# The last attention of two blocks: scores and values as products of rounded high and low parts

## What is computed

```python
def gqa_attend(q, k, v, sink=None):
    s = jnp.einsum('bqhgd,bkhd->bhgqk', q.reshape(b, tq, hkv, g, d), k).astype(jnp.float32) * d ** -0.5
    if sink is None:
        p = jax.nn.softmax(s, axis=-1)
    o = jnp.einsum('bhgqk,bkhd->bqhgd', p.astype(v.dtype), v)

# c_mixer: q_l, k_l rotated; k_all, v_all are context and latent tokens together (768)
    q_blocks = jnp.moveaxis(q_l.reshape(b, t // BLOCK, BLOCK, C_HEADS, C_HEAD_DIM), 1, 0)
    o = lax.map(lambda qb: gqa_attend(qb, k_all, v_all), q_blocks)
    y_lat = jnp.moveaxis(o, 0, 1).reshape(b, t, C_WIDTH) @ w_out
```

## Time and profile before

| | us |
|---|---|
| median of 3 runs | 2615.78 (2614.35 to 2617.09) |
| the profiled execution | 2614.36 |
| its span | 2612.6 |
| PE busy | 2381.1 (91%) |
| PE weight loads | 1929.9 (74%) |
| DVE busy | 1231.2 (47%) |
| ACT busy | 805.5 (31%) |
| POOL busy | 1003.8 (38%) |
| mean granted clock of PE | 0.954 |

### The profile page before, as it was taken

One profiled execution on the slowest core, in us unless ns is written; L12 is line 12 of the kernel. 1 busy time (PEld: TensorE's weight loads), 2 busy tenths in 40 slices (PEclk: granted clock), 3 DMA queues, 4 the chain that ended last, 5 costly groups with the idle time before them and its releaser, 6 DMA issues. The chain is left out here.

```text
span 2612.6 us, 34942 instructions
## 1 busy us (share of the span) xinstructions
PE 2381.1 (91%) x14323; PEld 1929.9 (74%) x14323; DVE 1231.2 (47%) x1956; ACT 805.5 (31%) x1325; POOL 1003.8 (38%) x606
## 2 busy tenths in 40 slices
PE   6987688999997989967789999999989998899998
PEld 5866466777775779855668888888867687688887
DVE  4417627756555660567436242332427752423432
ACT  4232334333335412335332111111134363322221
POOL 3326234655553322320136343443434002555553
PEclk8998898999997999979899999999989999899999
DMA  8570213444441111100113233333311101233221
GB/s 266 161 226 1 75 49 113 157 153 154 149 145 58 40 48 59 33 1 1 33 49 97 81 113 114 114 127 100 113 41 65 33 1 49 65 97 97 96 97 49
DMA packets 224700, 229.94 MB, mean 88 GB/s; under 512 B 7375, under 2 KB 221219, under 8 KB 224547
## 3 DMA queue, kind: packets, MB, share of 16 engines
q1 hardware_dynamic: 224211, 227.66, 27.1%
q10 hardware_dynamic: 336, 0.11, 0.0%
HBM read 225.65 MB, written 2.10 MB: 87 GB/s over the span
## 5 line engine op out<-in xcount | busy, mean ns | idle before, releaser
L1237 POOL TENSOR_TENSOR w_lo<-ring,w_hi 128x1024 fp32r<-128x1024 f32 x128 | 311.5, 2434 | 431.5 <-ACT w_hi L1232 431.5
L1232 ACT ACTIVATE w_hi<-ring 128x1024 fp32r<-128x1024 f32 x128 | 135.6, 1059 | 738.4 <-PE ps L1297 701.9
L2039 DVE SCALAR_TENSOR_TENSOR xT<-ps,mods,xT 128x512 f32<-128x512 f32 (+1 forms) x160 | 108.3, 683 | 533.0 <-PE ps L1297 474.0
L1295 PE MATMUL ps<-hidden_hi,w_hi 128*128 128x512 f32 (+1 forms) x768 | 273.9, 357 | 5.4 <-POOL hidden_lo L2393 5.4
L1296 PE MATMUL ps<-hidden_lo,w_hi 128*128 128x512 f32 (+1 forms) x768 | 272.1, 354 | 0.0
L1297 PE MATMUL ps<-hidden_hi,w_lo 128*128 128x512 f32 (+1 forms) x768 | 271.6, 354 | 0.0
L2316 DVE SCALAR_TENSOR_TENSOR ffn_sums<-ps,cols,ffn_sums 128x441 f32<-128x441 f32 (+2 forms) x352 | 215.0, 687 | 105.5 <-ACT ffn_sums L2237 105.5
L1295 PE MATMUL ps<-h_hi,w_hi 128*128 128x512 f32 (+1 forms) x720 | 256.4, 356 | 6.7 <-POOL w_lo L1237 3.0
L1296 PE MATMUL ps<-h_lo,w_hi 128*128 128x512 f32 (+1 forms) x720 | 255.0, 354 | 0.0
L1297 PE MATMUL ps<-h_hi,w_lo 128*128 128x512 f32 (+1 forms) x720 | 254.6, 354 | 0.0
L2383 DVE TENSOR_TENSOR squares<-squares 128x512 f32<-128x512 f32 (+1 forms) x72 | 144.9, 2013 | 217.7 <-ACT squares L2369 217.7
(11 more groups left out here) (448 smaller groups left out, 5223.7 us busy)
## 6 DMA issues: line engine op xcount, KB each, us to landing
ring<-in_mlp_w SPq DMA_DIRECT2D x64, 1024.0 KB, 5.3
ring<-in_ada_w SPq DMA_DIRECT2D x48, 1024.0 KB, 5.3
ring<-in_w_ada SPq DMA_DIRECT2D x24, 1024.0 KB, 9.6
ring<-in_ffn_w_up SPq DMA_DIRECT2D x22, 1024.0 KB, 7.0
ring<-in_ab_w_in SPq DMA_DIRECT2D x11, 1024.0 KB, 5.2
ring<-in_ffn_w_down SPq DMA_DIRECT2D x12, 768.0 KB, 6.0
ring<-in_w_in SPq DMA_DIRECT2D x8, 1024.0 KB, 7.5
ring<-in_c_w_in SPq DMA_DIRECT2D x6, 1024.0 KB, 5.0
```

The lines of the kernel that those rows point to most:

```text
L1232: act.activation(w_hi[m][:, 0:x["kt"], :], ring[:, x["n"] % NS, 0:x["kt"], m * P:(m + 1) * P], ACT.Copy).then_inc(SW["w_hi"].sem, 1)
L1237: pool.tensor_tensor(w_lo[m][:, 0:x["kt"], :], ring[:, x["n"] % NS, 0:x["kt"], m * P:(m + 1) * P], w_hi[m][:, 0:x["kt"], :].bitcast(F32), ...
L1295: pe.matmul(o, w_hi[m][:, k, :], h, start=(k == 0), stop=False)
L2039: return nc.vector.scalar_tensor_tensor(x, bank, column_of(gates, t * 2 + 2 * gate + r), x, ALU.mult, ALU.add)
```

## The change

`attention` becomes `split_attention`. The jobs and their order stay. Heads 1 to 7 make their scores from rounded parts, three products for each column range; head 0 keeps the float32 products. The values are made from rounded parts for two jobs (query blocks) at a time, with 256 columns. ACT's copy of the transposes, now rounded, is the high part `p_hi`; a new step `low(j)` on DVE subtracts it from the transposes in PSUM and writes `p_lo`, after `norm(j+1)` in DVE's queue. `turn(j)` waits for that step of job j-1 (`turned_v`) too. ACT rounds k, v and q of each head (`part_high`) at set steps of its loop, and POOL subtracts (`part_lo`). The low parts of q, k (but the first head's) and v are written over the originals. `scores(4h)` waits for the low parts of its head, `values` for those of v.

```diff
+            ops = [("v", 0), ("k", 0), ("q", 1), ("q", 2), ("v", 1), ("k", 1)] + [("q", h) for h in range(3, 8)]
+            when = {("v", 0): -1, ("k", 0): 0, ("v", 1): 7, ("k", 1): 8}
+            when.update({("q", h): 4 * h - 3 for h in range(1, 8)})
...
                 @block.gpsimd
                 def _(pool):
-                    for dst, factor in side:
-                        pool.tensor_tensor(dst, dst, factor, ALU.mult)
+                    for i, (kind, index) in enumerate(ops):
+                        x, hi, lo = tiles[kind](index)
+                        wait(pool, "part_hi", i + 1)
+                        sig(pool.tensor_tensor(lo, x, hi.bitcast(F32), ALU.subtract), "part_lo")
...
                         if j >= 2:
                             wait(pe, "exp", j - 1)
...
+                        if h and n == 0:
+                            wait(pe, "part_lo", max(ops.index(("q", h)), ops.index(("k", kv))) + 1)
+                        for c0, c1 in ((0, LAT), (LAT, TOK)):
+                            s_ps = flat[:, (j % 2) * 1024 + c0:(j % 2) * 1024 + c1]
+                            if h == 0:
+                                ins = pe.matmul(s_ps, qc[:, 0, q], kc[:, 0, c0:c1], start=True, stop=True)
+                            else:
+                                pe.matmul(s_ps, q_hi[:, h % 2, q], k_hi[:, kv, c0:c1], start=True, stop=False)
+                                pe.matmul(s_ps, q_hi[:, h % 2, q], keys_lo(kv)[:, c0:c1], start=False, stop=False)
+                                ins = pe.matmul(s_ps, q_lo[:, h, q], k_hi[:, kv, c0:c1], start=False, stop=True)
                         sig(ins, "qk")

                     def turn(j):
-                        width = jobs[j][2]
                         wait(pe, "norm", j + 1)
                         if j >= 1:
-                            wait(pe, "turned_out", j)
...
+                            wait(pe, "turned_a", j)
+                            wait(pe, "turned_v", j)
...
+                    def values(p):
+                        kv = p // (2 * NLAT)
+                        wait(pe, "turned_v", 2 * p + 2)
+                        wait(pe, "part_lo", ops.index(("v", kv)) + 1)
+                        if p >= 2:
+                            wait(pe, "pv_out", p - 1)
+                        o = ps[:, 6 + p % 2, 0:2 * P]
+                        for c in range(NCH):
+                            pe.matmul(o, v_hi[:, c, of_kv(kv)], p_hi[:, p % 2, c, :], start=(c == 0), stop=False)
+                            pe.matmul(o, v_hi[:, c, of_kv(kv)], p_lo[:, p % 2, c, :], start=False, stop=False)
+                            ins = pe.matmul(o, v_lo[:, c, of_kv(kv)], p_hi[:, p % 2, c, :],
+                                            start=False, stop=(c == NCH - 1))
                         sig(ins, "pv")
...
                         if j + 2 < n_jobs:
                             scores(j + 2)
                         turn(j)
-                        if j >= 1:
-                            values(j - 1)
-                    values(n_jobs - 1)
+                        if j >= 2 and j % 2 == 0:
+                            values(j // 2 - 1)
+                    values(n_pairs - 1)
...
+                    def low(j):
+                        wait(dve, "turned_a", j + 1)
+                        sig(dve.tensor_tensor(half(p_lo, j), turned_ps, half(p_hi, j).bitcast(F32), ALU.subtract), "turned_v")
...
                         if j + 1 < n_jobs:
                             top(j + 1)
                         norm(j)
+                        if j >= 1:
+                            low(j - 1)
+                    low(n_jobs - 1)
...
+                    part_high(-1)
                     expo(0)
                     for j in range(n_jobs):
                         if j + 1 < n_jobs:
                             expo(j + 1)
                         take(j)
-                        if j >= 1:
-                            give(j - 1)
-                    give(n_jobs - 1)
...
+                        if j >= 2 and j % 2 == 0:
+                            give(j // 2 - 1)
+                        part_high(j)
+                    give(n_pairs - 1)
```

More of the change, by code:

```diff
@@ L2513, in rope, with split_attention, parts @@
                 R[n].close(len(tiles))
-        def attention(jobs, scale, bufs, side=()):
-            sc, pt, stat = bufs
-            R = named("qk", "top", "max", "exp", "norm", "turned", "turned_out", "pv", "pv_out")
+        def split_attention(qc, kc, vc, out_t, sc, stat, scale, space):
+            n_jobs, n_pairs = 8 * NLAT, 4 * NLAT
+            at = [space]
+            def parts(name, shape):
+                at[0] += 4 * math.prod(shape[1:])
+                return rounded(name, at[0] - 4 * math.prod(shape[1:]), shape)
+            p_hi, p_lo = parts("p_hi", [P, 2, NCH, 2 * P]), parts("p_lo", [P, 2, NCH, 2 * P])
+            k_hi, k0_lo = parts("k_hi", [P, 2, TOK]), parts("k0_lo", [P, TOK])
+            v_hi, q_hi = parts("v_hi", [P, NCH, SLAB]), parts("q_hi", [P, 2, LAT])
+            q_lo = rounded("q_lo", big_at, [P, 8, LAT])
+            k_lo = rounded("k_lo", big_at + 4 * 8 * LAT, [P, 2, TOK])
+            v_lo = rounded("v_lo", big_at + 4 * (8 * LAT + 2 * TOK), [P, NCH, SLAB])
+            of_kv = lambda kv: slice(kv * P, (kv + 1) * P)
+            keys_lo = lambda kv: k0_lo[:, :] if kv == 0 else k_lo[:, 1, :]
+            ops = [("v", 0), ("k", 0), ("q", 1), ("q", 2), ("v", 1), ("k", 1)] + [("q", h) for h in range(3, 8)]
+            when = {("v", 0): -1, ("k", 0): 0, ("v", 1): 7, ("k", 1): 8}
+            when.update({("q", h): 4 * h - 3 for h in range(1, 8)})
+            tiles = {"v": lambda i: (vc[:, :, of_kv(i)], v_hi[:, :, of_kv(i)], v_lo[:, :, of_kv(i)]),
+                     "k": lambda i: (kc[:, i, :], k_hi[:, i, :], keys_lo(i)),
+                     "q": lambda i: (qc[:, i, :], q_hi[:, i % 2, :], q_lo[:, i, :])}
+            R = named("qk", "top", "max", "exp", "norm", "turned", "turned_a", "turned_v", "pv", "pv_out", "part_hi", "part_lo")
             sig = lambda ins, n: ins.then_inc(R[n].sem, 1)
@@ L2524, in attention @@
             flat = ps[:, :, :].rearrange("p b n -> p (b n)")
-            n_jobs = len(jobs)
+            turned_ps = flat[:, 2048:2048 + TOK].rearrange("p (c n) -> p c n", c=NCH)
+            half = lambda buf, j: buf[:, (j // 2) % 2, :, (j % 2) * P:(j % 2 + 1) * P]
             with nc.Block() as block:
@@ L2534, in scores @@
                     def scores(j):
-                        q, keys, _, _, _, _ = jobs[j]
+                        h, n = divmod(j, NLAT)
+                        kv, q = h // 4, slice(n * CH, (n + 1) * CH)
                         if j >= 2:
                             wait(pe, "exp", j - 1)
[L2538 to L2542, removed]
+                        if h and n == 0:
+                            wait(pe, "part_lo", max(ops.index(("q", h)), ops.index(("k", kv))) + 1)
@@ L2553, in turn @@
+                            wait(pe, "turned_v", j)
+                        for c in range(NCH):
+                            ins = pe.transpose(turned_ps[:, c, :], sc[:, j % 2, c * P:(c + 1) * P], ident)
                         sig(ins, "turned")
[L2555 to L2563, removed]
+                    def values(p):
[5 more added lines that the diff above has]
+                        o = ps[:, 6 + p % 2, 0:2 * P]
+                        for c in range(NCH):
+                            pe.matmul(o, v_hi[:, c, of_kv(kv)], p_hi[:, p % 2, c, :], start=(c == 0), stop=False)
+                            pe.matmul(o, v_hi[:, c, of_kv(kv)], p_lo[:, p % 2, c, :], start=False, stop=False)
+                            ins = pe.matmul(o, v_lo[:, c, of_kv(kv)], p_hi[:, p % 2, c, :],
+                                            start=False, stop=(c == NCH - 1))
@@ L2587, in top @@
                             wait(dve, "exp", j - 1)
[L2588 to L2592, removed]
+                        sig(dve.tensor_scalar(m, t, -scale, None, ALU.mult), "max")
                     def norm(j):
-                        _, _, width, _, sink, _ = jobs[j]
                         b = j % 2
+                        den = stat[:, b, 1:2]
                         wait(dve, "exp", j + 1)
-                        den = stat[:, b, 1:2]
-                        if sink is not None:
-                            v_order.step(dve, dve.tensor_tensor(den, den, stat[:, b, 2:3], ALU.add))
                         v_order.step(dve, dve.reciprocal(den, den))
-                        sig(dve.tensor_scalar(sc[:, b, 0:width], sc[:, b, 0:width], den, None, ALU.mult), "norm")
+                        sig(dve.tensor_scalar(sc[:, b, 0:TOK], sc[:, b, 0:TOK], den, None, ALU.mult), "norm")
+                    def low(j):
+                        wait(dve, "turned_a", j + 1)
+                        sig(dve.tensor_tensor(half(p_lo, j), turned_ps, half(p_hi, j).bitcast(F32), ALU.subtract), "turned_v")
                     top(0)
```

(19 more changed lines are left out.)

15 lines of the change are left out of this document (6 added, 9 removed).

## The result

The changed kernel takes 2652.3 us (median of 4 runs, 2647.2 to 2655.0) against 2616.4: its time is 1.0129 times that of before, 95% interval 1.0115 to 1.0143. That is 36 us more, where 32 were forecast (2648, range 2632 to 2668).

What follows compares the result with a forecast made beforehand. The prediction took PE to bound the stage. To 2614.4 us it added 10.6 (DVE's low part, start and end), 11.8 (waits for q) and 11 (slow clock), 2647.8, said as 2648 us, range 2632 to 2668.

Steps and rivals of the forecast that it cites:

- PE's own work: PE's work for two jobs: 5.54 us in place of 6.58, 15.6 us less in all if PE stayed the bound.
- The circle through DVE's low part: Steady loop: transposes wait for the previous job's low part; two jobs take 6.96 us in place of 6.58, +8.0 us.
- One sign: PE's waits in the stage would name DVE's subtraction some 15 times, with about 1.4 us each.
- The end of the stage: From the last transposes to the last copy: 5.5 us in place of 3.87, +1.6 us.
- the sum of +10.6: Steady loop +8.0 us, interval of jobs 0 and 1 +1.0, end of the stage +1.6.
- The late parts of q: Scores of heads 1 to 7 wait for POOL's low part: seven intervals of 4.74 us for 3.11, +11.8 us in all.
- The clock: Behind the seven waits for q, PE's clock falls five times at 2.2 us each: +11 us (0 to +25).
- The case of 2.95 us of idle time without a fall: Rival: clock stays at 1.00 in the seven waits, as at 2258.87 in the earlier trace; 2637 us, chance 0.20.
- the clock also falls in the steady circles: Rival: slow clock in the steady loop too, for half of 15 rounds, +31 us; 2667 us, chance 0.18.
- the wait for DVE hides: Rival: PE's wait for the low part is hidden and the kernel gets faster, 2599 to 2604 us, chance 0.08.
- GpSimd beside DVE: POOL's subtractions disturbing DVE's divisions in the stage: priced at nothing, up to +5 us.
- circle and ends: Steady loop waiting for DVE's low part, plus start and end of the stage: +10.6 us.

Runs made afterwards that it cites:

- e3: The changed kernel with float32 scores for all heads and no parts of q and k; stage 122.9 us, 1.0054 of before.
- e5: e1 with each pair's values cut in two, three key blocks behind the even transposes and three behind the odd; stage 106.9 us, 0.9998 of before.
- e8: e1 with DVE subtracting only three of the six blocks of the low part, used twice by the values; stage 115.7 us.
- e1: The changed kernel with ACT rounding q of each head two jobs earlier (head 1 in step 0); stage 122.5 us, 1.0049 of before.
- e2: The changed kernel with six extra float32 products on PE ahead of each of the seven waits for q; stage 132.6 us, 1.0086 of before.
- e7: Rounded scores with values as before the change, and q rounded as late as in the changed kernel; stage 128.1 us, one run of 2637.8 us.

## Why the prediction was right

**PE's own work.** Right. 18 products of the values go from 2090.82 to 2093.07, 2.25 us, where 2.16 was forecast (the first takes 0.21); the scores 1.05. A pair is thus 5.65 us of PE work where 5.54 was forecast. PE has less to do, 91 us busy in 120, and the stage is longer.

**The circle through DVE's low part.** Right in its mechanism and size: 6.98 us for two jobs, 6.96 forecast. The low part takes 954 ns on average (0.96 forecast, from a copy of 640 columns and a maximum over 768). Two small errors cancel: DVE runs its round in 2.73 us, from 2087.34 to 2090.07, since the next instruction starts a little before the last one's end, and the handover to PE takes 0.15 in place of 0.05. e3 shows the circle alone, e5 cuts it by moving half of the values out of it, and e8 shortens it by shortening DVE's instruction; each came out as its own sum. One sign was counted too high: PE waits for the low part in the loop of the changed kernel not some 15 times but in seven pairs (1.22 us) and beside them in the first and the last two jobs, since where it waits for q the low part is ready by then.

The end of the stage was the term that was too small. From the last transposes to the end of the last copy it takes 7.04 us (6.88 in e1), 3.2 more than before, where 1.6 was forecast: PE waits 1.89 for the last low part, and the values behind it run at a clock of 0.50, which the sum of +10.6 did not hold.

**The late parts of q.** Right: waits of 2.85 to 3.04 us at seven places, 3.05 forecast. The sum was 4.74 us between the two transposes; in e2, at full clock, it is 4.74 to 4.77, and 4.95 at head 3, where 0.4 was added in the forecast and 0.2 came. Against 3.08 that is 11.9 us for the seven, 11.8 forecast. In the changed kernel itself the interval is 4.99 (2094.12 to 2099.11), with the start of the slow clock in it.

**The clock.** Right in sum, 11.9 us by e2 against 11, but partly by luck, for two errors in its parts cancel: I had five falls of seven at 2.2 us. There were seven of seven, at 1.6 each (11.3), and 0.5 at the end. The case of 2.95 us of idle time without a fall did not come; each of the waits had a stretch at 0.50 behind it. It was not certain, though: with idle times of 2.32 us in e7 it was five of seven. That stretch begins after PE has gone on, at 2098.6 in the case above, so that it falls on dense work. e2 shows that its cost is real and not time in which PE would have waited.

**The rivals.** That the clock also falls in the steady circles did not happen: in e1 it is 1.00 for 104 us, with one idle time of 1.2 us in nearly every pair. That the wait for DVE hides did not happen either. It all but does in e5, with 5.89 us for two jobs, and DVE's rounds are then nearly the bound, as that rival said. But the stage takes 106.9 us in place of 96. The steady pairs give back 9.7 us (14 x 0.69); head 1, with its wait and slow stretch, and head 3 cost 3.3 of it, the first pair 1.0, the last pair, in which PE has no scores left, 1.6, and the end 1.7.

**GpSimd beside DVE.** Priced at nothing, and nearly that: the division takes 644 ns on average where it took 620, 0.8 us for 32 of them. It is not spread evenly: two divisions beside POOL's subtractions for k (0.89 and 1.12 us) make up all of it, and in e1 the one of 1.14 us is the whole excess at head 3. The low part of 768 columns keeps its 952 to 954 ns in e1, e5 and the changed kernel, also beside POOL. This agrees with what the Trainium skill (SBUF — State Buffer, Who interferes with whom) says of instructions with one SBUF input.

The sum, with the circle and ends as what is left of 35.7 (144.5 - 108.8): circle and ends 11.9 (10.6 forecast), waits for q 11.9 (11.8), clock 11.9 (11); 35.7 in place of 33.4.

## What to carry to other kernels

A count of work by engine says how long a stage could be; how long it is, the circles say: follow each new wait from the waiting engine round through what stands behind it in that queue until it comes back to itself, and add it up. Here PE was given some 14 us less to do (28 scores at 1.05 us in place of 1.30, 16 pairs of values at 2.25 in place of 2.68), and a DVE step of 0.96 us that closed a circle with two jobs' values inside it took back more than that (e3, e1); the same instructions in another order (e5) lost nothing. Parts that another engine must make belong so early in its queue that the user's queue never gets to the wait; a wait of 3 us on TensorE made the stage 1.7 us longer by itself and another 1.6 by the slow clock behind it.

## What the runs showed of the hardware

- Seven idle times of TensorE of 2.85 to 3.04 us, each in otherwise dense work, all had a stretch at 1.2 GHz behind them, which began after the engine had gone on. One of 2.95 us in the trace of before had none. The length of the idle time alone does not tell the two apart: of the seven of 2.32 us in e7 five had a slow stretch behind them and two had none, one of 2.33 in e1 had none, one of 2.06 in e5 had one. With the idle time filled by products that nobody reads (e2) there was no slow stretch at these places, and the stage was 11.9 us shorter.
- Idle times of 1.2 us, one in nearly every 7 us, and once 2.33 us, over 104 us: the clock stayed at 2.4 GHz (e1).
- A DVE instruction that writes 768 columns was followed by the next after 0.87 us where its own record says 0.95 (2089.12 to 2089.99), so a DVE round is shorter than the sum of its records.
- A DVE division (768 columns, SBUF to SBUF) that started while GpSimd subtracted 768 columns ended 0.41 to 0.43 us behind that subtraction, whatever its own start: it took 0.62 us where it began late in it, 1.14 (e1) and 1.33 (e5) where it began early. A GpSimd subtraction of 512 columns that started 0.17 us behind a division took 1.61 us in place of 1.27 (e1). DVE's subtraction with one input in PSUM and one in SBUF kept 0.94 to 0.96 beside GpSimd.
